# Four modulation parts beside the latent attention: products on GpSimd and sums on ScalarE in place of matmuls on TensorE

## The reference, cut to what matters

```
sc = jax.nn.silu(c)                                        # 1024 values
shift1, scale1, gate1, shift2, scale2, gate2 = jnp.split(sc @ w_mod[l] + b_mod[l], 6, axis=-1)
cmods = jnp.split(scc @ w_mod[l][:, :2 * D_MODEL] + ..., 2, axis=-1)
h = modulate(rms_norm(x, norm1_g[l]), shift1, scale1)
y, yc = token_mixer(h, hc, P, last)                        # holds the latent attention, 8 heads
x = x + gate1[:, None, :] * y
h = modulate(rms_norm(x, norm2_g[l]), shift2, scale2)
x = x + gate2[:, None, :] * grouped_moe(h, ...)
```

## Time and profile before

| | |
|---|---|
| median of 3 runs | 2278.57 us (2278.43 to 2285.46) |
| span of the profiled execution | 2270.7 us |
| what lies around the span (median less span) | 7.9 us |
| TensorE matmul busy | 2091.7 us, 92% |
| VectorE busy | 1109.4 us, 49% |
| ScalarE busy | 858.0 us, 38% |
| GpSimd busy | 574.2 us, 25% |
| mean granted TensorE clock | 0.968 |
| the latent attention's stage | 311.6 us to about 452.8 us of the span |

### The profile page before, as it was taken

One profiled execution on the slowest core, in us unless ns is written; L12 is line 12 of the kernel. 1 busy time (PEld: TensorE's weight loads), 2 busy tenths in 40 slices (PEclk: granted clock), 3 DMA queues, 4 the chain that ended last, 5 costly groups with the idle time before them and its releaser, 6 DMA issues. The chain is left out here.

```text
span 2270.7 us, 23562 instructions
## 1 busy us (share of the span) xinstructions
PE 2091.7 (92%) x9502; PEld 1588.8 (70%) x9502; DVE 1109.4 (49%) x1334; ACT 858.0 (38%) x1067; POOL 574.2 (25%) x191
## 2 busy tenths in 40 slices
PE   6998999999879999789999979999799997999997
PEld 3766755474358888578777757787688876878886
DVE  3345546545780224468888567305702246223223
ACT  4441223334222223457777547514422323212221
POOL 1421300130014445020000123440144444443441
PEclk9999999999989999989999989999899999999999
DMA  7223224231014323289999932231022332322310
GB/s 246 93 94 143 93 93 133 91 111 33 0 37 141 99 86 121 75 306 388 365 385 384 332 134 93 79 106 35 20 93 88 98 121 93 111 93 74 97 51 38
DMA packets 174671, 299.16 MB, mean 132 GB/s; under 512 B 8900, under 2 KB 66443, under 8 KB 174569
## 3 DMA queue, kind: packets, MB, share of 16 engines
q1 hardware_dynamic: 169256, 279.40, 35.9%
q0 software_dynamic: 3008, 9.93, 1.2%
q10 hardware_dynamic: 2304, 8.39, 0.9%
HBM read 274.57 MB, written 23.13 MB: 131 GB/s over the span
## 5 line engine op out<-in xcount | busy, mean ns | idle before, releaser
L130 POOL TENSOR_TENSOR region<-weights,region 128x2048 fp32r<-128x2048 f32 (+2 forms) x94 | 367.1, 3907 | 992.6 <-ACT region L124 746.0
L240 PE MATMUL ps<-region 128*128 128x512 f32 (+1 forms) x1336 | 528.7, 396 | 42.5 <-DVE region L570 12.7
L244 PE MATMUL ps<-region 128*128 128x512 f32 (+1 forms) x1336 | 518.2, 388 | 0.0
L243 PE MATMUL ps<-region 128*128 128x512 f32 (+1 forms) x1336 | 518.0, 388 | 0.0
L240 PEld LDWEIGHTS ps<-region 128*128 128x128 f32 x1336 | 258.2, 193 | 104.9 <-DVE region L130 25.5
L243 PEld LDWEIGHTS ps<-region 128*128 128x128 f32 x1336 | 258.2, 193 | 52.4 <-issue 4.1
L244 PEld LDWEIGHTS ps<-region 128*128 128x128 f32 x1336 | 257.6, 193 | 49.9
L124 ACT ACTIVATE region<-weights 128x2048 fp32r<-128x2048 f32 (+2 forms) x98 | 158.5, 1621 | 289.0 <-PE ps L244 235.0
L2960 DVE TENSOR_TENSOR region<-weights,region 128x2048 fp32r<-128x2048 f32 x92 | 209.3, 2288 | 48.1 <-ACT region L2869 47.7
L2869 ACT ACTIVATE region<-weights 128x2048 fp32r<-128x2048 f32 x92 | 176.1, 1917 | 69.4 <-DMA weights<-moe_w_up 29.3
L281 PE MATMUL ps<-region 128*128 128x512 f32 x480 | 190.1, 396 | 7.2 <-DVE region L4063 4.6
(11 more groups left out here) (441 smaller groups left out, 2704.4 us busy)
## 6 DMA issues: line engine op xcount, KB each, us to landing
weights<-w_in SPq DMA_DIRECT2D x54, 1024.0 KB, 5.3
weights<-moe_w_gate SPq DMA_DIRECT2D x32, 1024.0 KB, 7.9
weights<-moe_w_up SPq DMA_DIRECT2D x32, 1024.0 KB, 8.8
weights<-moe_w_down SPq DMA_DIRECT2D x32, 1024.0 KB, 7.7
weights<-w_mod SPq DMA_DIRECT2D x24, 1024.0 KB, 5.4
weights<-w_mlp_in SPq DMA_DIRECT2D x16, 1024.0 KB, 5.2
weights<-w_mlp_out SPq DMA_DIRECT2D x16, 1024.0 KB, 5.0
h_slots<-region SPq DMA_DIRECT2D x16, 512.0 KB
```

The source lines that it names most:

```text
L130: eng.tensor_tensor(flat(self.part(K, n, 1)), flat(self.ring.view(n)), flat(self.part(K, n, 0)).bitcast(F32), ALU.subtract).then_inc(self. ...
L240: ins = pe.matmul(out, l_hi, r_hi, start=(start and k == 0), stop=False)
L243: pe.matmul(out, l_hi, r_lo, start=False, stop=False)
L244: ins = pe.matmul(out, l_lo, r_hi, start=False, stop=(stop and k == kt - 1))
```

## The change

`w_mod`'s last four parts are laid out transposed by the host (`w_mod_rows`, 4096 x 1024), so that each output value's 1024 weights lie in one partition. `c` is loaded into all 128 partitions (`sc_row`, 512 KB) in `qk_stage`, and ScalarE applies silu to it there. In the latent attention GpSimd multiplies one tile of 128x1024 weights by `sc_row` (32 tiles, into three buffers in turn), ScalarE sums each product along its row with an activation in place that accumulates, and one VectorE instruction at the end of the stage adds `b_mod` to all 32 columns. TensorE and the PSUM bank drop out. The number of ring chunks stays 16.

```diff
-    def pe(self, pe, a):
-        ...
-            mod_products(K, pe, a % 4, K.ring.view(n), self.BANK).then_inc(K.ring.used, 1)
-        if a % 4 == 3 and g < self.GROUPS:
-            pe.wait_ge(self.rows_copied, g + 1)
-            mod_turn(K, pe, self.rows, self.BANK, 0).then_inc(self.turned, 1)
-    def act(self, act, a):
-        if a % 4 == 2 and a // 4 < self.GROUPS:
-            ...
-            act.activation(self.rows, self.K.ps[:, self.BANK, :], ACT.Copy).then_inc(self.rows_copied, 1)
-    def dve(self, dve, a):
-        ...
+    CHUNKS, TILES, AT = 16, 32, (48, 52, 68)
+    def product(self, j):
+        return self.K.at(self.AT[j % 3], D)
+
+    def pool(self, pool):
+        r = self.K.ring
+        for j in range(self.TILES):
+            n = self.n0 + j // 2
+            if j % 2 == 0:
+                pool.wait_ge(r.arrived[n % RING], r.arrival(n))
+            if j >= 3:
+                pool.wait_ge(self.summed, j - 2)
+            pool.tensor_tensor(self.product(j), r.view(n)[:, j % 2, :], self.K.sc_row, ALU.mult)\
+                .then_inc(*((r.used, 1) if j % 2 else (self.multiplied, 1)))
+
+    def act(self, act, j):
+        if j < self.TILES:
+            act.wait_ge(*((self.K.ring.used, self.n0 + j // 2 + 1) if j % 2 else (self.multiplied, j // 2 + 1)))
+            act.activation(self.product(j), self.product(j), ACT.Copy, accum_out=self.raw[:, j:j + 1])\
+                .then_inc(self.summed, 1)
+
+    def dve(self, dve):
+        K, j0 = self.K, 16
+        dve.wait_ge(self.summed, self.TILES)
+        ...
+        dve.tensor_tensor(self.m[:, j0:j0 + self.TILES, 0], self.raw, bm, ALU.add).then_inc(self.added, 1)
 # qk_stage
+            sp.dma_start(K.sc_row, T["c"].broadcast_to([P, D])).then_inc(c_in, 16)
             r.issue_until(sp, n0 + 6 + RING)
         ...
+                if q == 0:
+                    act.wait_ge(c_in, 16)
+                    act.activation(K.sc_row, K.sc_row, ACT.Silu).then_inc(c_ready, 1)
 # attention_stage
         def _(pool):
+            if beside:
+                beside.pool(pool)
             for n in first:
                 split.low(K, pool, n)
 # plan_block1
-    for g in range(4, 12):
-        for h in range(2):
-            r.add("mod2", wm[h][:, :, g * HALF:(g + 1) * HALF])
+    for n in range(LaterMods.CHUNKS):
+        r.add("mod2", T["w_mod_rows"][256 * n:256 * (n + 1), :].rearrange("(t p) c -> p t c", p=P))
```

More of the change, by code:

```diff
@@ L432 @@
 class LaterMods:
-    GROUPS = 8
-    BANK = 7
+    CHUNKS, TILES, AT = 16, 32, (48, 52, 68)
     def __init__(self, K, signals, kb):
-        self.K, self.rows = K, K.at(kb, HALF)
-        self.rows_copied, self.turned, self.added = signals[:3]
+        self.K, self.raw = K, K.at(kb, self.TILES)
+        self.multiplied, self.summed, self.added = signals[:3]
         self.n0 = K.ring.first("mod2")
         self.m = K.mods[:, :].rearrange("p (j b) -> p j b", b=2)
-    def pe(self, pe, a):
[L448 to L453, removed]
-            mod_products(K, pe, a % 4, K.ring.view(n), self.BANK).then_inc(K.ring.used, 1)
-        if a % 4 == 3 and g < self.GROUPS:
-            pe.wait_ge(self.rows_copied, g + 1)
-            mod_turn(K, pe, self.rows, self.BANK, 0).then_inc(self.turned, 1)
@@ L459, in act @@
-    def act(self, act, a):
-        if a % 4 == 2 and a // 4 < self.GROUPS:
-            g = a // 4
-            act.wait_ge(self.K.ring.used, self.n0 + 2 * g + 2)
-            act.activation(self.rows, self.K.ps[:, self.BANK, :], ACT.Copy).then_inc(self.rows_copied, 1)
-    def dve(self, dve, a):
[L466 to L479, removed]
+    def product(self, j):
+        return self.K.at(self.AT[j % 3], D)
@@ new lines, in dve @@
+    def dve(self, dve):
+        K, j0 = self.K, 16
+        dve.wait_ge(self.summed, self.TILES)
+        bm = K.vecs[:, VEC_AT["b_mod"] + j0:VEC_AT["b_mod"] + j0 + self.TILES]
+        dve.tensor_tensor(self.m[:, j0:j0 + self.TILES, 0], self.raw, bm, ALU.add).then_inc(self.added, 1)
+        dve.wait_ge(self.added, 1)
+        g2 = K.vecs[:, VEC_AT["norm2_g"]:VEC_AT["norm2_g"] + 8]
+        dve.scalar_tensor_tensor(K.gain2, self.m[:, 32:40, 0], 1.0, g2, ALU.add, ALU.mult).then_inc(self.added, 1)
+        dve.wait_ge(self.added, 2)
@@ L830, in _ @@
             act.wait_ge(rows_done, 2)
+            act.wait_ge(c_ready, 1)
         @block.vector
@@ L1505, in _ @@
                     ins.then_inc(s_done, 1)
-                if beside:
-                    beside.pe(pe, a)
                 b = a - 2
@@ L1548, in _ @@
             for a in range(NB + 2):
-                if beside:
-                    beside.dve(dve, a)
                 if a < NB:
@@ L1574, in _ @@
                     dve.tensor_copy(PT[:, h % 2, :, (b % ST) * P:(b % ST + 1) * P], tbank()).then_inc(copied, 1)
+            if beside:
+                beside.dve(dve)
 def latent_attention_stage(K):
@@ L4160 @@
            "w_mlp_out_2"]
-ROWS = ["gla_norm_g", "hy_decay", "hy_skip", "router_b"]
+ROWS = ["c", "gla_norm_g", "hy_decay", "hy_skip", "router_b"]
 def layout(inputs):
@@ L4176, in layout @@
         np.stack([np.asarray(inputs[n]).reshape(-1) for n in ("hy_pos_b1", "hy_pos_b2", "hy_sin_freq")], axis=1))
+    out["w_mod_rows"] = np.ascontiguousarray(np.asarray(inputs["w_mod"])[0][:, 2 * D:].T)
     out["vecs"] = np.ascontiguousarray(
@@ L4269, in plan_block1 @@
             r.add("mod", w[h][:, :, g * HALF:(g + 1) * HALF])
-    wm, w = w, T["w_in"]
+    w = T["w_in"]
     r.add_matrix("ga", w, C_GA, C_GA + P)
@@ L4370, in block1_stages @@
     K.hid = K.at(134, S)[0:64]
[L4371 removed]
+    K.rstd_x, K.rstd_c, K.sc_row = K.at(90, S), K.at(92, NCTX), K.at(64, D)
     return [
```

3 lines of the change are left out of this document (1 added, 2 removed).

## The result

The changed kernel takes **2302.59 us** (median of 4 runs, 2299.74 to 2307.83), the kernel before beside it 2279.61 (4 runs, 2278.43 to 2285.46): ratio 1.0101, 95% interval 1.0086 to 1.0117. It is 23 us, 1.0%, slower. The forecast was 2314, range 2293 to 2334.

The account below looks back on a forecast made before the run. The prediction took the chain to each exponential, ending with VectorE's bias, as the bound, not TensorE's busy time. Span 2270.7 + 26 (holds) + 9 (clock) = 2305.7, plus 7.9 around it: 2314 us, range 2293 to 2334.

Parts of the forecast that it names:

- held, clock never falls: Case for the attention: GpSimd's products hold the bias while TensorE's clock stays up; 2305 us, chance 0.3.
- What leaving TensorE is worth, 7 us: Attention without the modulation products on TensorE: a head at best 15.5 us against 16.4, 7 us over eight heads.
- The bias is held, though no row showed it: VectorE's softmax bias, two one-element SBUF inputs, waits for the rest of a running GpSimd product, up to 2.35 us.
- Nothing is held: Rival for the attention: bias passes GpSimd, scaling runs between products, a head takes 15.5 us; 2272 us, chance 0.04.
- only the scaling is held: Rival for the attention: bias passes, the scaling's stall is partly hidden, a head takes 17.5 us; 2288 us, chance 0.13.
- The round of 4.64: Ordinary attention interval between exponentials, with the bias held by a product: 4.64 us in place of 2.8 to 3.4.
- The pair of 10.2: Two exponential intervals of a head, around L263's multiplication by the values: stay 10.2 us, one bias's delay hidden there.
- The first four blocks, exponential 4 at 21.8 us into the stage: Start of the attention: three products run without waiting for a sum; block 4's exponential comes 6.5 us later than before.
- 26 us at an unchanged clock: Attention's loss without clock effects: 6.5 for the first blocks, 6 x 3.1 for heads, 1 for the tail.
- The clock term, 9 us: TensorE idles in attention rounds, its clock falls and L263 slows: 18 us if always, nothing if never, half taken.
- The tail, +1: Last attention blocks: last biases free, next stage's subtractions one product later, a held scaling partly freed; +1 us.
- The sum, 35 us: Added to the whole kernel's span: 26 us in the attention at an unchanged clock and 9 us for TensorE's clock.

Follow-up runs that it names:

- e4: Changed kernel with products and sums over 16 of 1024 columns (modulation values wrong): 2270.29 us, ratio 0.9953 to the kernel before.
- e1: Changed kernel with the softmax row maximum in PSUM, so the bias has one SBUF input: 2280.85 us, ratio 1.001 to the kernel before.
- e3: Changed kernel with products and sums over 512 of 1024 columns (modulation values wrong): 2272.14 us, ratio 0.9969 to the kernel before.
- e6: Changed kernel with full products, each made to wait for VectorE's work in its round: 2274.32 us, ratio 0.998 to the kernel before.
- e5: Changed kernel with eight more TensorE matmul rows, results unused, in three of four rounds: 2304.24 us, ratio 1.011 to the kernel before.
- the fair pair: One run each of the changed kernel and of the kernel before with 32 GpSimd memsets added: 2309.07 and 2279.29 us.
- e2: Changed kernel with row maximum and reciprocal in PSUM, scaling as tensor_tensor with one SBUF input: 2270.33 us, ratio 0.9961 to the kernel before.
- e7: Changed kernel with products waiting for VectorE's work and the row maximum in PSUM: 2272.06 us, ratio 0.9974 to the kernel before.

## Why the prediction came out as it did

The direction and the mechanism were right; the time was 11 us too high, within the range. The measured 2303 lies nearest to the case "held, clock never falls" (2305), which the traces refute: the clock fell (0.86) and cost 7 us. What brought the number down lies outside the stage.

- *What leaving TensorE is worth, 7 us:* right, 7.0 in e4; the head of 15.5 us was 15.52.
- *The product, 2.35 us:* 2.357.
- *The bias is held, though no row showed it:* shown. It stands in the changed trace, vanishes with one operand moved (e1), shrinks with the product's length (e3), and with the product's place (e6). "Nothing is held" and "only the scaling is held" both fall, for the changed kernel.
- *The round of 4.64:* 4.59 to 4.67. *The pair of 10.2:* 4.67 and 5.55 make 10.22 where the clock stays up (10.21 in e5). *A head of 19.5:* 19.46.
- *The first four blocks, exponential 4 at 21.8 us into the stage:* 333.03 - 311.84 = 21.2, so they cost 5.9 us in place of 6.5. The holds came in the order given: the biases of blocks 0 and 1, the first scaling (2.60 us), the bias of block 2. GpSimd's first products run back to back, as assumed; after's timeline:

```profile
311.82 11.89 POOL L455 TENSOR_TENSOR region<-weights,region 128x1024 f32<-128x1024 f32 x5 [28.79 <-POOLq L644]
...
333.03 0.99 ACT L1530 ACTIVATE region<-ps,region 128x768 f32<-128x768 f32 x1 [2.54 <-DVE region L1555]
```

- *26 us at an unchanged clock:* 272.9 - 245.9 = 27.0 in e5. By the exponentials these are 5.9 for the first blocks, 18.8 for six heads (18.6) and 2.3 behind exponential 28, where I had taken 1.
- *The clock term, 9 us:* 7.1, after against e5. It was the guess of a half between never and always; four of six steady heads paid 1.5 to 1.8 us each, and none showed the full 2.6.
- *Loads, silu, tables at nothing:* the attention starts 311.84 - 208.0 = 103.8 us behind the first stretch's start, before 311.60 - 207.8 = 103.8. Nothing.
- *The tail, +1:* 2.3 in e5 (from exponential 28 to the end of the first stretch 31.05 us against 28.71). The step that failed in it is "GpSimd ends its 32nd product after block 28, so the last biases are free": the last product ran from 458.70 to 461.05 and held the bias of block 29, 2.10 us. The last L263 took 7.35 at a low clock as before, and the one addition on VectorE, held to 2.44 us, lay under it.
- *The sum, 35 us:* 34.1. That it is right to 1 us is in part luck: the first blocks and the clock came out 0.6 and 1.9 us lower, the heads and the tail 0.2 and 1.3 higher. What failed is the step from the stage to the kernel: "The median and this sum rest on the same base". It took for granted that the rest of the program stays as it is. One gap behind the overflow stage is 4.3 to 4.5 us shorter, for a cause that isn't shown. About 7 us more, between 29.8 in the fair pair and 23 in the medians, can't be assigned: the parts ahead of and behind the stage move by about 5 us each from run to run, and four runs of after against four of before don't average that out.
- The 7.9 us "around the span" were wrong as a thing: 1.8 lies there (2299.74 - 2297.9). Before's profile was simply a short run beside its median. The forecast used the median, so this cost nothing.

Three variants that do the whole work beat both kernels by more than the interval, e2, e6 and e7, at 0.4, 0.2 and 0.3% under before. Only e7 gains in the stage of the change itself (242.4 against 245.9 us); e2 (246.2) and e6 (246.5) are level there, so their 9 and 5 us are the gap's 4.3 and a rest that isn't assigned.

## What to carry to other kernels

Before work goes to an idle GpSimd, list VectorE's instructions on the critical path beside it, the small ones too: here one of 0.16 us was held for up to 2.17 us by a 2.36 us product. A product that is released by the same round as the instruction meets it again and again, here in three rounds of four. Moving one operand to PSUM, or starting the product behind the sensitive instruction, took back nearly all of it (31 and 33.5 of 34 us). And a stage's sum can be right to 1 us while two profiles of one kernel differ by 5 to 9 in the whole: compare stage by stage, and give the total from runs.

## What was not expected of the hardware

- TensorE's clock fell in four of six steady heads and not in the other two, though their rounds ahead of L263 were alike to 0.1 us (granted 0.86 over the stage). Eight more matmul rows in three of four rounds kept it at 0.96. What decides between the heads stays open.
- A scaling of 128x768 takes 620 ns as `tensor_scalar` on SBUF and is held by GpSimd; as `tensor_tensor` with its factor in PSUM it takes 953 ns and isn't. Which is better depends on the neighbour's place in the round: e7 keeps the first form, mean 788 ns with its holds, and has the shorter head (15.8 against 16.57 us).
- The hyena stage has about three lengths (211.6 to 217.1 us, granted clock 0.96 to 0.93) over these profiles, and two of them (213.7 and 217.0) with one kernel. It goes against what lies ahead: the four profiles with 217 us reached the first stretch at 208.4 to 208.6 us, and all eight that reached it at 210.5 or later have 211.6 to 213.7.
